# The first expert pair's up and down places, released and refilled in halves

## The chip, the cores and the metric

The kernel runs on one core of a Trainium2 chip. The metric is the device time of one launch in microseconds (us), as the median of several executions. Inputs are float32.

## What is computed

Two transformer blocks on one sequence of 256 tokens with a width of 1024. The change touches only the last part of the second block, its mixture of experts. Every token is sent to 2 of 32 experts, and each expert has three matrices of 2 MB (1024 x 512, 1024 x 512 and 512 x 1024), 201 MB in all:

```python
def _hierarchical_moe(h, w_group, w_expert, w_gate, w_up, w_down):
    ...
    def expert_block(args):
        xb, e = args
        return (jax.nn.silu(xb @ w_gate[e]) * (xb @ w_up[e])) @ w_down[e]

    y = lax.map(expert_block, (buf.reshape(n_blocks, MOE_BLOCK, d), block_expert)).reshape(cap, d)
    contrib = y[dest] * w_sorted[:, None].astype(y.dtype)
    return jnp.zeros((n, d), y.dtype).at[tok_sorted].add(contrib)
```

The result is scaled by a gate, added to the residual and normalised.

## The kernel before

The program is written out by hand for each engine, with semaphores between them. SP (SyncE) issues the loads of the weights in one fixed order, each behind a wait for the engine that frees its place; PE does the products; ACT and DVE evacuate, activate and scale; POOL does small work.

The 32 experts are taken as 16 pairs, since two experts with 64 token slots each share the 128 rows of TensorE. PE's part of pair p is `pair` in the tensor program. It does, in this order: the gate product (line 1389, 16 matmul calls, shown as 32 instructions), which ends in an increment of `s_eg`; the up product (line 1405), which ends in `s_eu`; the dispatch of the tokens of pair p + 1 (line 1333); transposes of the activated rows (line 1413); the combine of pair p - 1 (line 1350, from pair 1 on); transposes for the combine weights (line 1419); and the down product (line 1433), which ends in `s_edn`. ACT's `tokens` (line 1728) and DVE's (line 2313) copy the dispatched tokens, and ACT's line 1740 copies the transposed rows that the down product reads.

The weights lie in ten places of 16 KB per partition (`eslots`) and in one that is used a single time (`used_once`). `matrix(c, n)` is matrix c (0 gate, 1 up, 2 down) of expert n, so matrix (1,4) is the up matrix of expert 4, in pair 2. `matrix_number` counts them in the order of use, `slot_of` gives the place of each, and `requests_until` tells how many DMAs into that place must have landed before matrix m may be read (each DMA adds 16 to the place's `loaded` semaphore). `into` issues one whole load of 2 MB (line 666). Each load into a place waits until the matrix before it in the place is used up: for (1,7), for instance, until `s_edn` tells that pair 1's down product is done.

The first pair is special. Its gate product releases its two places in quarters: after every second of its eight k steps it adds one to `s_part`, SP waits for each count, and `quarter_into` (line 673) refills a quarter of each place, with matrices (2,3) and (0,4). [...] The up and down places of the first pair are refilled whole: (0,5) and (1,4) after `s_eu`, (1,5) and (2,4) after `s_edn`. The last pair's up and down matrices are loaded in halves (`halves_of_last`, line 692), and its down product adds a count to `s_part` when one of its two output halves is done, for which DVE waits.

The loads around the change, in SP's order, each behind the semaphore that it waits for: (2,3) and (0,4) `s_part` 1 to 4; (0,5), (1,4) `s_eu` 1; (1,5), (2,4) `s_edn` 1; (2,5), (0,6) `s_eg` 2; (0,7), (1,6) `s_eu` 2; (1,7) `s_edn` 2; (2,6), (2,7) `s_eg` 3; (0,8), (0,9) `s_eu` 3; (1,8), (1,9) `s_edn` 3; (2,8), (2,9) `s_eg` 4; and so on, six loads a pair.

Of the kernel before, what the change touches and what calls it, by code (L numbers as in the profile page):

```python
# [19 lines left out]
def two_block_kernel(nc, a, out):  # L20
# [22 lines left out]
    KE = FE // P  # L43
# [27 lines left out]
    ESLOT_N = 10  # L71
# [3 lines left out]
    QUARTERS = 4  # L75
# [16 lines left out]
    with ctx:  # L92
# [391 lines left out]
        def slot_of(m):  # L484

            if m == ESLOT_N:
                return ONCE
            return ESLOTS[m if m < ESLOT_N else (m - 1) % ESLOT_N]

        def requests_until(m):  # L490

            if m == ESLOT_N:
                return 2
            before_experts = N_MOE // LANES if slot_of(m) < LANES else 0
            in_quarters = QUARTERS - 1 if m > ESLOT_N and slot_of(m) in (slot_of(ESLOT_N + 1), slot_of(ESLOT_N + 2)) \
                else 0
            uses = 1 if m < ESLOT_N else (m - 1) // ESLOT_N + 1
            return before_experts + in_quarters + uses
# [5 lines left out]
        def expert_slot(u, c, e):  # L504

            return slot_of(matrix_number(u, c, e))
# [89 lines left out]
        def _(sp):  # L596
# [71 lines left out]
            def quarter_into(slot, src, quarter):  # L668

                rows = src.shape[1] // QUARTERS  # L670
                dst = expert_place(slot).rearrange("p (k n) -> p k n", k=src.shape[1])
                part = slice(quarter * rows, (quarter + 1) * rows)
                sp.dma_start(dst[:, part, :], src[:, part, :]).then_inc(loaded[slot], 16)
# [34 lines left out]
            for quarter in range(QUARTERS):  # L708
                sp.wait_ge(s_part, quarter + 1)
                quarter_into(expert_slot(1, 2, 1), matrix(2, 3), quarter)  # L710
                quarter_into(expert_slot(2, 0, 0), matrix(0, 4), quarter)
            into(expert_slot(2, 0, 1), matrix(0, 5), (s_eu, 1))
            into(expert_slot(2, 1, 0), matrix(1, 4), None)
            into(expert_slot(2, 1, 1), matrix(1, 5), (s_edn, 1))
            into(expert_slot(2, 2, 0), matrix(2, 4), None)
# [149 lines left out]
        def _(pe):  # L865
# [492 lines left out]
            def pair(p, u, r=None, last_one=False):  # L1358
# [48 lines left out]
                last.then_inc(s_eu, 1)  # L1407
# [21 lines left out]
                for f, c in order:  # L1429
# [6 lines left out]
                    if last_one and c == 0 and f == KE - 1:  # L1436
                        last.then_inc(s_part, 1)
                last.then_inc(s_edn, 1)
# [330 lines left out]
        def _(ve):  # L1769
# [546 lines left out]
            def pair(p, last_one=False):  # L2316
# [33 lines left out]
                if last_one:  # L2350
                    ve.wait_ge(s_part, QUARTERS + 1)
# [86 lines left out]
```

## Time and profile before

| | |
|---|---|
| Median of 3 runs | 1024.78 us |
| Lowest and highest | 1024.5 and 1026.88 us |
| The profiled execution's own time | 1026.15 us |
| Its span, first to last instruction | 1024.5 us |
| Mean granted TensorE clock over the span | 0.991 of full |
| Busy: PE, weight loads, DVE, ACT, POOL | 97%, 68%, 54%, 34%, 8% |
| Read from HBM | 310.47 MB |

The page cuts the span into 40 slices of 25.6 us; the expert stage fills those from the 23rd on. A timeline row has the start and the length of a group of instructions of one line, in us, and behind it in brackets the idle time of the engine before it and what ended that. Since matmuls overlap, the modelled end of a group can lie a little behind the start of the next. SP's rows are DMA issues: the time is that of the issue, not of the transfer. A DMA answer gives the time from the issue of a load to its landing, when all of it is in place.

### The profile page before, as it was taken

What the parts mean: (1) busy time and instruction counts of PE and PEld (TensorE: products, weight loads), DVE (VectorE), ACT (ScalarE), POOL (GpSimd) and SP (SyncE); (2) the same over time, 40 slices, a digit from 0 to 9 for tenths busy, and PEclk for the clock granted to TensorE, in tenths of its full rate; (3) what the DMA queues carried; (4) which work ended last, traced back from release to release, by engine and by line L of the source; (5) the groups of instructions that cost most, each with busy time, mean ns of one, the idle gap of its engine ahead of it and who ended that gap; (6) DMA issues with size and microseconds to landing.
All of it is one profiled execution on the core that took longest, in us unless ns stands there. A gap on an engine that the chain in (4) does not pass through costs nothing.

```text
span 1024.5 us, 15516 instructions
## 1 busy us (share of the span) xinstructions
PE 997.0 (97%) x6010; PEld 699.2 (68%) x6010; DVE 551.8 (54%) x1043; ACT 343.3 (34%) x572; POOL 79.6 (8%) x118
## 2 busy tenths in 40 slices
PE   8998999999999999999999999999999999999997
PEld 6897789989999998989965544444444444443442
DVE  8556689799899997748533622222222222222222
ACT  5555664464444554427250311111011111110112
POOL 7200110011011200300001000000000000000000
PEclk9999999999999999899999999999999999999999
DMA  8334176797879864245665899999999999999994
GB/s 299 123 124 164 46 257 237 264 345 276 307 300 320 301 219 164 83 166 208 265 265 176 317 361 429 423 429 428 427 427 427 427 427 429 429 427 428 429 424 190
DMA packets 60006, 312.15 MB, mean 305 GB/s; under 512 B 4117, under 2 KB 5498, under 8 KB 47418
## 3 DMA queue, kind: packets, MB, share of 16 engines
q1 hardware_dynamic: 52160, 284.83, 69.5%
q0 software_dynamic: 7392, 26.54, 7.2%
q8 instruction: 32, 0.52, 0.2%
q10 hardware_dynamic: 410, 0.16, 0.1%
q14 instruction: 12, 0.10, 0.0%
HBM read 310.47 MB, written 1.05 MB: 304 GB/s over the span
## 4 chain that ended last, share of the span: by engine, by line
PE 78%; DMA 8%; DVE 7%; issue 3%; ACT 2%; POOL 0%; DVEq 0%; SPq 0%
PE bank L1433 10%; PE bank L1405 10%; PE bank L1389 9%; PE bank L898 9%; PE bank L899 9%; PE bank L900 9%; PE bank L1333 6%; DMA eslots<-in_w_up 3%; DMA ring<-in_w_up 3%; PE bank L1045 3%; PE bank L1350 3%; DVE ring_r L1850 2%; DMA ring<-in_w_in 2%; PE bank L973 1%; PE bank L1011 1%
## 5 line engine op out<-in xcount | busy, mean ns | idle before, releaser
L898 PE MATMUL bank<-hT_r,ring_r 128*128 128x256 f32 x664 | 190.0, 286 | 2.7 <-DVE ring_r L1850 2.7
L900 PE MATMUL bank<-hT_r,ring_r 128*128 128x256 f32 x664 | 188.4, 284 | 0.0
L1850 DVE TENSOR_TENSOR ring_r<-ring,ring_r 128x2048 fp32r<-128x2048 f32 (+1 forms) x74 | 164.4, 2257 | 14.6 <-ACT ring_r L1511 14.2
L1511 ACT ACTIVATE ring_r<-ring 128x2048 fp32r<-128x2048 f32 (+1 forms) x74 | 136.5, 1888 | 37.4 <-DMA ring<-in_w_up 32.6
L899 PE MATMUL bank<-v_tok_r,ring_r 128*128 128x256 f32 x496 | 140.4, 283 | 0.0
L898 PEld LDWEIGHTS bank<-hT_r,ring_r 128*128 128x128 f32 x664 | 128.0, 193 | 4.0 <-issue 2.4
L900 PEld LDWEIGHTS bank<-hT_r,ring_r 128*128 128x128 f32 x664 | 127.9, 193 | 0.0
L1405 PE MATMUL bank<-eslots,scratch 128*64 128x512 f32 x512 | 114.5, 600 | 3.0 <-DMA eslots<-in_w_up 2.1
L1433 PE MATMUL bank<-eslots,scratch 128*64 128x512 f32 x496 | 113.5, 595 | 0.7 <-ACT scratch L1740 0.7
L1389 PE MATMUL bank<-eslots,scratch 128*64 128x512 f32 x512 | 112.7, 592 | 0.0
L899 PEld LDWEIGHTS bank<-v_tok_r,ring_r 128*128 128x128 f32 x496 | 95.2, 192 | 0.2
L2329 DVE TENSOR_TENSOR scratch<-scratch,bank 128x512 f32<-128x512 f32 x16 | 11.0, 688 | 156.5 <-PE bank L1405 156.5
L1405 PEld LDWEIGHTS bank<-eslots,scratch 128*64 128x64 f32 x512 | 38.6, 138 | 76.8 <-issue 73.9
L900 PE MATMUL bank<-ring_r,hn_r 128*128 128x512 f32 (+2 forms) x240 | 88.9, 370 | 0.0
L1389 PEld LDWEIGHTS bank<-eslots,scratch 128*64 128x64 f32 x512 | 37.1, 137 | 72.2 <-issue 72.1
L1433 PEld LDWEIGHTS bank<-eslots,scratch 128*64 128x64 f32 x496 | 35.6, 137 | 63.1 <-issue 61.3
L2341 DVE SCALAR_TENSOR_TENSOR scratch<-bank,scratch,post_ffn 128x512 f32<-128x512 f32 x32 | 22.6, 746 | 99.8 <-PE bank L1433 99.8
L1744 ACT ACTIVATE scratch_r<-scratch 128x512 fp32r<-128x512 f32 x32 | 20.2, 630 | 148.5 <-DVE scratch L2341 148.0
L1333 PEld LDWEIGHTS bank<-scratch,hn 128*128 128x128 f32 x512 | 58.4, 192 | 12.7 <-issue 12.2
L779 POOL TENSOR_TENSOR small<-small 128x1 f32<-128x1 f32 (+1 forms) x20 | 15.1, 758 | 638.2 <-DVE small L2402 453.0
L1728 ACT ACTIVATE scratch<-bank,small 128x128 f32<-128x128 f32 x64 | 18.2, 368 | 132.9 <-PE bank L1333 132.9
L1333 PE MATMUL bank<-scratch,hn 128*128 128x128 f32 x512 | 61.4, 278 | 0.0
(306 smaller groups left out, 1470.2 us busy)
## 6 DMA issues: line engine op xcount, KB each, us to landing
eslots<-in_w_gate SPq DMA_DIRECT2D x31, 2048.0 KB, 23.6
eslots<-in_w_up SPq DMA_DIRECT2D x30, 2048.0 KB, 18.8
eslots<-in_w_down SPq DMA_DIRECT2D x28, 2048.0 KB, 22.5
ring<-in_w_up SPq DMA_DIRECT2D x16, 2048.0 KB, 11.1
ring<-in_w_in SPq DMA_DIRECT2D x9, 2048.0 KB, 7.9
ring<-in_w_down SPq DMA_DIRECT2D x8, 2048.0 KB, 8.5
kT<-in_w_ada POOLq DMA_DIRECT2D x24, 512.0 KB, 7.2
ring<-in_w_out SPq DMA_DIRECT2D x4, 2048.0 KB, 8.2
```

The costliest lines, as they stand in the source:

```text
L898: pe.matmul(dst, lhs[0], rhs[0], start=start, stop=False, **flags)
L899: pe.matmul(dst, lhs[0], rhs[1], start=False, stop=False, **flags)
L900: return pe.matmul(dst, lhs[1], rhs[0], start=False, stop=stop, **flags)
L1045: last = pe.matmul(PS[PROJ_BANKS[1][t, c]][:, :], hT[:, k, t * P:(t + 1) * P], w[:, k % HALF_K, c * HALF:(c + 1) * HALF], start=(first and ...
L1333: last = pe.matmul(XB[k // 4][:, (k % 4) * P:(k % 4 + 1) * P], hn[:, t, k * P:(k + 1) * P], oneh[:, t, :], start=(t == 0), stop=(t == T - 1))
L1350: last = pe.matmul(ACC[2 * t + c][:, :], combT[:, t, :], ye[:, part, c * HALF:(c + 1) * HALF], start=False, stop=False, skip_group_check=True)
L1389: last = pe.matmul(GB[64 * e:64 * e + 64, :], xeT[:, k, 64 * e:64 * e + 64], weights(0, e, k), start=(k == 0), stop=(k == KD - 1))
L1405: last = pe.matmul(UB[64 * e:64 * e + 64, :], xeT[:, k, 64 * e:64 * e + 64], weights(1, e, k), start=(k == 0), stop=(k == KD - 1))
L1433: last = pe.matmul(XB[c][64 * e:64 * e + 64, :], eactT[:, f, 64 * e:64 * e + 64], weights(2, e, f)[:, c * HALF:(c + 1) * HALF], start=(f = ...
L1511: sc.activation(hi, raw, ACT.Copy).then_inc(s_whi, 1)
L1850: last = ve.tensor_tensor(lo, raw, hi, ALU.subtract)
L2341: ve.scalar_tensor_tensor(ye_sum[:, half], PS[4 + c][:, :], wslot, post_ffn[:, half], ALU.mult, ALU.mult).then_inc(s_yg, 1)
```

## The change

The first pair's up product raises `s_part` after k steps 3 and 7, its down product after f steps 1 and 3 (in each the second column half's matmul), so that `s_part` counts to eight in that pair. PE then waits for count six and raises `s_eu` with a nop, and for count eight and raises `s_edn` with a nop. SP waits for counts five and six and loads halves of (0,5) and (1,4), two DMAs of 1 MB behind each count; then for seven and eight, with halves of (1,5) and (2,4). `quarter_into` becomes `part_into` with the number of parts, `requests_until` counts one more DMA for the four places, and DVE's wait in the last pair goes from count five to nine.

```diff
-            in_quarters = QUARTERS - 1 if m > ESLOT_N and slot_of(m) in (slot_of(ESLOT_N + 1), slot_of(ESLOT_N + 2)) \
-                else 0
+            in_parts = 0
+            if m > ESLOT_N:
+                in_parts = {slot_of(ESLOT_N + 1): QUARTERS - 1, slot_of(ESLOT_N + 2): QUARTERS - 1,
+                            slot_of(ESLOT_N + 3): 1, slot_of(ESLOT_N + 4): 1,
+                            slot_of(ESLOT_N + 5): 1, slot_of(ESLOT_N + 6): 1}.get(slot_of(m), 0)
...
-            into(expert_slot(2, 0, 1), matrix(0, 5), (s_eu, 1))
-            into(expert_slot(2, 1, 0), matrix(1, 4), None)
-            into(expert_slot(2, 1, 1), matrix(1, 5), (s_edn, 1))
-            into(expert_slot(2, 2, 0), matrix(2, 4), None)
+            for half in range(2):
+                sp.wait_ge(s_part, QUARTERS + half + 1)
+                part_into(expert_slot(2, 0, 1), matrix(0, 5), half, parts=2)
+                part_into(expert_slot(2, 1, 0), matrix(1, 4), half, parts=2)
+            for half in range(2):
+                sp.wait_ge(s_part, QUARTERS + half + 3)
+                part_into(expert_slot(2, 1, 1), matrix(1, 5), half, parts=2)
+                part_into(expert_slot(2, 2, 0), matrix(2, 4), half, parts=2)
             into(expert_slot(2, 2, 1), matrix(2, 5), (s_eg, 2))
...
-                last.then_inc(s_eu, 1)
+                    if isinstance(p, int) and p == 0 and k % 4 == 3:
+                        last.then_inc(s_part, 1)
+                if isinstance(p, int) and p == 0:
+                    pe.wait_ge(s_part, QUARTERS + 2)
+                    pe.nop().then_inc(s_eu, 1)
+                else:
+                    last.then_inc(s_eu, 1)
...
-                    if last_one and c == 0 and f == KE - 1:
+                    first_pair_half = isinstance(p, int) and p == 0 and c == 1 and f % 2
+                    if (last_one and c == 0 and f == KE - 1) or first_pair_half:
                         last.then_inc(s_part, 1)
-                last.then_inc(s_edn, 1)
+                if isinstance(p, int) and p == 0:
+                    pe.wait_ge(s_part, QUARTERS + 4)
+                    pe.nop().then_inc(s_edn, 1)
+                else:
+                    last.then_inc(s_edn, 1)
...
-                    ve.wait_ge(s_part, QUARTERS + 1)
+                    ve.wait_ge(s_part, QUARTERS + 5)
```

SP's queue from the last quarter on, before the change (the name behind "waits" is the semaphore that the issue waits for):

```order
L673 DMA eslots<-in_w_gate 128x1024
L666 DMA eslots<-in_w_gate 128x4096 [waits s_eu]
L666 DMA eslots<-in_w_up 128x4096
L666 DMA eslots<-in_w_up 128x4096 [waits s_edn]
L666 DMA eslots<-in_w_down 128x4096
L666 DMA eslots<-in_w_down 128x4096 [waits s_eg]
```

And with the change (the lines are numbered three higher):

```order
L676 DMA eslots<-in_w_gate 128x1024
L676 DMA eslots<-in_w_gate 128x2048 [waits s_part]
L676 DMA eslots<-in_w_up 128x2048
L676 DMA eslots<-in_w_gate 128x2048 [waits s_part]
L676 DMA eslots<-in_w_up 128x2048
L676 DMA eslots<-in_w_up 128x2048 [waits s_part]
L676 DMA eslots<-in_w_down 128x2048
L676 DMA eslots<-in_w_up 128x2048 [waits s_part]
L676 DMA eslots<-in_w_down 128x2048
L669 DMA eslots<-in_w_down 128x4096 [waits s_eg]
```

Four whole loads have become eight of half the size, behind four waits instead of two; the load of (2,5) and all that follow it stand where they stood.

PE in the first pair, from the up product to the next pair's gate, before the change:

```order
L1405 MATMUL bank<-eslots,scratch 64x512 x15
L1333 MATMUL bank<-scratch,hn 128x128 [waits s_oneh,s_yV]
L1333 MATMUL bank<-scratch,hn 128x128 x15
L1413 MATMUL bank<-ident,scratch 128x128 [waits s_eact]
L1413 MATMUL bank<-ident,scratch 128x128 x3
L1419 MATMUL bank<-ident,scratch 128x128 [waits s_onehw]
L1419 MATMUL bank<-ident,scratch 128x128
L1433 MATMUL bank<-eslots,scratch 64x512 [waits loaded7,s_xeV,loaded1,s_xeA,s_eactT]
L1433 MATMUL bank<-eslots,scratch 64x512 x15
L1389 MATMUL bank<-eslots,scratch 64x512 [waits loaded6,loaded2,s_eactT,s_xeA]
```

And with it:

```order
L1412 MATMUL bank<-eslots,scratch 64x512 x15
L1340 MATMUL bank<-scratch,hn 128x128 [waits s_part,s_oneh,s_yV]
L1340 MATMUL bank<-scratch,hn 128x128 x15
L1426 MATMUL bank<-ident,scratch 128x128 [waits s_eact]
L1426 MATMUL bank<-ident,scratch 128x128 x3
L1432 MATMUL bank<-ident,scratch 128x128 [waits s_onehw]
L1432 MATMUL bank<-ident,scratch 128x128
L1446 MATMUL bank<-eslots,scratch 64x512 [waits loaded7,s_xeV,loaded1,s_xeA,s_eactT]
L1446 MATMUL bank<-eslots,scratch 64x512 x15
L1396 MATMUL bank<-eslots,scratch 64x512 [waits s_part,loaded6,loaded2,s_eactT,s_xeA]
```

No matmul moves. The dispatch and the next gate product each stand behind one more wait, the one for `s_part`.

## Rows read from the trace of the kernel before

**Rows 1.** The page: PE's busy time, and GB/s in the 40 slices

```profile
PE 997.0 (97%) x6010; PEld 699.2 (68%) x6010; DVE 551.8 (54%) x1043; ACT 343.3 (34%) x572; POOL 79.6 (8%) x118
...
GB/s 299 123 124 164 46 257 237 264 345 276 307 300 320 301 219 164 83 166 208 265 265 176 317 361 429 423 429 428 427 427 427 427 427 429 429 427 428 429 424 190
```

**Rows 2.** Timeline of PE, gate and up of pair 2

```profile
633.68 7.04 PE L1389 MATMUL bank<-eslots,scratch 128*64 128x512 f32 x32
640.54 7.04 PE L1405 MATMUL bank<-eslots,scratch 128*64 128x512 f32 x32
```

**Rows 3.** Timeline of PE, pair 0 and the gate of pair 1

```profile
580.09 7.09 PE L1389 MATMUL bank<-eslots,scratch 128*64 128x512 f32 x32
587.49 7.09 PE L1405 MATMUL bank<-eslots,scratch 128*64 128x512 f32 x32 [0.32 <-PE bank L1389]
594.51 3.84 PE L1333 MATMUL bank<-scratch,hn 128*128 128x128 f32 x32
...
599.73 7.09 PE L1433 MATMUL bank<-eslots,scratch 128*64 128x512 f32 x32 [0.72 <-ACT scratch L1740]
606.62 7.07 PE L1389 MATMUL bank<-eslots,scratch 128*64 128x512 f32 x32
```

**Rows 4.** DMA issued at 667.78, 949.57 and 976.42: size, us to landing

```profile
eslots<-in_w_down SPq DMA_DIRECT2D x1, 2048.0 KB, 11.6
...
eslots<-in_w_gate SPq DMA_DIRECT2D x1, 2048.0 KB, 39.7
...
eslots<-in_w_down SPq DMA_DIRECT2D x1, 1024.0 KB, 32.7
```

**Rows 5.** Timeline of PE, up of pairs 12 to 14, down of pair 15

```profile
911.04 7.09 PE L1405 MATMUL bank<-eslots,scratch 128*64 128x512 f32 x32
...
940.36 8.78 PE L1405 MATMUL bank<-eslots,scratch 128*64 128x512 f32 x32 [2.08 <-DMA eslots<-in_w_up]
...
969.77 7.09 PE L1405 MATMUL bank<-eslots,scratch 128*64 128x512 f32 x32 [0.48 <-issue]
...
1007.33 7.24 PE L1433 MATMUL bank<-eslots,scratch 128*64 128x512 f32 x32
```

**Rows 6.** Windows: busy us (x), granted clock, DMA share, GB/s

```profile
606.00:610.00 4.00, 4.00 (x20) 1.56 (x18) 3.04 (x7) 1.26 (x2) 0.00 (x0) 1.00 0.60 164
594.00:597.00 3.00, 3.00 (x26) 2.49 (x23) 0.69 (x1) 0.40 (x2) 0.00 (x0) 1.00 0.89 254
```

**Rows 7.** Timeline of SP: issues of (1,4), (1,5), (2,6) and (1,8)

```profile
594.98 0.43 SPq L666 DMA_DIRECT2D eslots<-in_w_up  x1
...
606.85 0.33 SPq L666 DMA_DIRECT2D eslots<-in_w_up  x1
...
640.75 1.06 SPq L666 DMA_DIRECT2D eslots<-in_w_down  x2
...
660.92 0.81 SPq L666 DMA_DIRECT2D eslots<-in_w_up  x2
```

**Rows 8.** DMA issued at 594.98, 606.85, 640.75, 660.92, then 529.24, 562.70

```profile
eslots<-in_w_up SPq DMA_DIRECT2D x1, 2048.0 KB, 12.8
...
eslots<-in_w_up SPq DMA_DIRECT2D x1, 2048.0 KB, 7.8
...
eslots<-in_w_down SPq DMA_DIRECT2D x1, 2048.0 KB, 9.0
...
eslots<-in_w_up SPq DMA_DIRECT2D x1, 2048.0 KB, 8.6
...
eslots<-in_w_down SPq DMA_DIRECT2D x1, 2048.0 KB, 7.5
...
eslots<-in_w_gate SPq DMA_DIRECT2D x1, 2048.0 KB, 7.8
```

**Rows 9.** Windows, as rows 6: after the idle time before 940.36

```profile
940.00:944.00 4.00, 3.64 (x10) 1.18 (x12) 0.00 (x0) 0.00 (x0) 0.00 (x0) 0.59 1.00 426
```

More of the change, by code:

```diff
@@ L494, in requests_until @@
             before_experts = N_MOE // LANES if slot_of(m) < LANES else 0
-            in_quarters = QUARTERS - 1 if m > ESLOT_N and slot_of(m) in (slot_of(ESLOT_N + 1), slot_of(ESLOT_N + 2)) \
-                else 0
+            in_parts = 0
[3 more added lines that the diff above has]
+                            slot_of(ESLOT_N + 5): 1, slot_of(ESLOT_N + 6): 1}.get(slot_of(m), 0)
             uses = 1 if m < ESLOT_N else (m - 1) // ESLOT_N + 1
-            return before_experts + in_quarters + uses
+            return before_experts + in_parts + uses
         def matrix_number(u, c, e):
@@ L666, in into, with part_into @@
                 sp.dma_start(dst, src).then_inc(loaded[slot], 16)
-            def quarter_into(slot, src, quarter):
-                rows = src.shape[1] // QUARTERS
+            def part_into(slot, src, n, parts=QUARTERS):
+                rows = src.shape[1] // parts
                 dst = expert_place(slot).rearrange("p (k n) -> p k n", k=src.shape[1])
-                part = slice(quarter * rows, (quarter + 1) * rows)
+                part = slice(n * rows, (n + 1) * rows)
                 sp.dma_start(dst[:, part, :], src[:, part, :]).then_inc(loaded[slot], 16)
@@ L709, in _ @@
                 sp.wait_ge(s_part, quarter + 1)
-                quarter_into(expert_slot(1, 2, 1), matrix(2, 3), quarter)
-                quarter_into(expert_slot(2, 0, 0), matrix(0, 4), quarter)
-            into(expert_slot(2, 0, 1), matrix(0, 5), (s_eu, 1))
-            into(expert_slot(2, 1, 0), matrix(1, 4), None)
-            into(expert_slot(2, 1, 1), matrix(1, 5), (s_edn, 1))
-            into(expert_slot(2, 2, 0), matrix(2, 4), None)
+                part_into(expert_slot(1, 2, 1), matrix(2, 3), quarter)
+                part_into(expert_slot(2, 0, 0), matrix(0, 4), quarter)
+            for half in range(2):
[6 more added lines that the diff above has]
+                part_into(expert_slot(2, 2, 0), matrix(2, 4), half, parts=2)
             into(expert_slot(2, 2, 1), matrix(2, 5), (s_eg, 2))
```

## The prediction

> **What bounds the kernel now.** I read the page first. PE is busy in 97% of the span, which by itself would say that only PE's work counts, but from the 25th slice to the 39th (from some 615 us) the DMA engines move 423 to 429 GB/s without a break [rows 1]. So the expert stage, which begins near 576 us, has two near-bounds. The timeline of PE gives the first: in a pair that waits for nothing the gate product starts 27.06 us after the one of the pair before (606.62, 633.68) [rows 2, 3]. The DMA answers give the second: the load issued at 667.78 landed after 11.6 us, at 679.4, and the one issued at 949.57 after 39.7, at 989.3 [rows 4]. Between them lie 63 loads of 2 MB (three of the same pair, then ten pairs of six), so one takes 309.9 / 63 = 4.92 us, and a pair's six 29.5 us. The DMA is 2.5 us a pair slower than PE, and PE lives on a head start that it uses up. The timeline near the end shows where that is gone [rows 5]: the up products at 940.36 and 969.77 start after 2.08 us (for DMA) and 0.48 us of idle time, and the last down product takes 7.24 us where 7.09 is usual, because its last half lands at 976.42 + 32.7 = 1009.1, just when it is wanted [rows 3 to 5]. **So the end of this kernel is set by when the stream of loads ends.** A us taken out of an early hole of the stream is a us at the end, if it stays out, up to a limit: PE by itself would start the product of 969.77 at 911.04 + 2 x 27.06 = 965.2, some 4.6 us earlier.
>
> **The holes.** The windows show two that the change aims at [rows 6]. From 606 to 610 us the DMA moved 164 GB/s where 428 is usual: 4 x (1 - 164/428) = 2.5 us missing. The queue had run dry, and the next load was issued only at 606.85, when the first pair's down product ended. From 594 to 597 it moved 254: 3 x (1 - 254/428) = 1.2 us. The busy share is 0.89 there, so part of it is the slow start of a new transfer.
>
> **Part 1: halves into the places of the first up.** Matrices (0,5) and (1,4) are issued when the up product ends, the second at 594.98 [rows 3, 7]. After the change their first halves go out when half of that product is done, 587.49 + 3.55 = 591.0, the second halves at 594.6. The quarters before them keep the engines busy until about 595, so the stream has no hole there: up to 1.2 us gained.
>
> **Part 2: halves into the places of the first down.** The first halves of (1,5) and (2,4) go out at 599.73 + 3.55 = 603.3 (plus the wait of part 4) instead of 606.85, while earlier loads still run. (1,4) landed at 594.98 + 12.8 = 607.8 and (1,5) at 606.85 + 7.8 = 614.7 [rows 7, 8]: 6.9 us between two landings where 4.9 is usual, so up to 2.0 us gained.
>
> **Part 3: smaller transfers.** Halves of 1 MB exist at the end of the kernel: the last eight take from 989.3 to 1009.1, 19.8 us for 8 MB, which four whole loads move in 19.7 [rows 4]. So eight more halves cost the stream 0.1 us, at most 0.3. SP issues eight DMAs in place of four, at 0.33 to 0.43 us each [rows 7]; that is hidden, as SP waits for PE between them.
>
> **Part 4: two new waits on PE.** After the first pair's up and its down product PE waits for its own last increment before a nop passes on `s_eu` and `s_edn`. The gate product has such a wait already: up starts 0.31 us after the gate's end (580.09 + 7.09), and 7.40 us after its start, against 6.86 in a later pair (633.68, 640.54) [rows 2, 3]. So it costs 0.54 there. Without a wait the dispatch starts 0.07 us before up's modelled end (594.51 against 594.58) and the next gate 0.20 us before down's (606.62 against 606.82). With 0.31 us behind the end they start 0.38 and 0.51 us later: **0.89 us in all**. The bounds are nothing, if a wait is over when PE reaches it, and 2 x 0.54 = 1.08. Behind these waits stand the dispatch, the transposes and the down product of PE, ACT's and DVE's tokens, which wait for the dispatch, and every later pair; PE has no idle time to absorb it until the stage's end. There it costs nothing by itself: PE waits 2.08 + 0.48 us for loads anyway.
>
> **Part 5: what becomes of the gain.** Loads (1,5) and (2,4) come up to 3.0 us earlier (1.2 + 2.0 - 0.2). But a later load is issued when PE frees its place, and PE is 0.89 us later, not earlier. So I follow each load as the later of two times: the landing before it + 4.9, and its own issue + what a load takes from a queue that has run dry. That second price is 7.5, 7.8 and 7.8 us in three rows [rows 8]; I take 7.8, that of 606.85, the nearest in time and an up matrix too. (2,4) lands at 616.6, 3.0 earlier. (2,6), issued at 640.75 + 0.89 = 641.6, can't land before 649.4; it was 640.75 + 9.0 = 649.8. So nearly all of the gain is lost again in a new hole: there was no free place to load into. (0,9), three loads on, lands at 664.1. (1,8), issued at 660.92 + 0.89 = 661.8, can't land before **669.6; it was 669.5** (8.6 after its issue, little more than from a dry queue) [rows 7, 8]. From there every load waits 5 us or more in the queue, PE's pace no longer matters to it, and the stream keeps what it has: 0.1 us later than before.
> The bounds: with 7.5 us (1,8) lands 0.2 earlier than it did; with waits that cost nothing it lands between 668.4 and 668.7, 0.8 to 1.1 earlier; with 1.08 us of waits 0.3 later.
> The Trainium skill (DMA: Bandwidth & Descriptors, Anatomy of one DMA) puts a transfer at about 2.0 us of fixed time plus its bytes at 436 GB/s, 6.8 us for 2 MB; the trace doesn't agree, with 7.5 to 7.8. By the page (1,8) would land at 668.6, and the sum would be 0.9 us faster instead of 0.1 slower.
>
> **Sum.** +0.1 us on the profiled execution's 1026.15 (1.65 of which lie around its span of 1024.5). That execution stands 1.4 us over the median of the runs shown; on the median of 1024.78 the forecast is **1024.9 us**. A measurement of this kernel can tell about 0.3% (3.1 us) from no change, and this is far inside.
>
> **The rivals.**
> A. *The holes stay closed.* If a load into a nearly dry queue landed 5 us after its issue, the 3.0 us would reach the end: 1021.8. For it: PE has the waits to give back. Against it: no row has less than 7.5, and PE frees the places no earlier. Chance 0.06, half of it beyond 0.3%.
> B. *The waits or the restart are cheaper.* With nothing for the waits 0.9 us is left at the end: 1023.9; with 0.89 of waits and the quickest landing 1024.6. For it: part of the gate's 0.54 may belong to its own place. Against it: up began 0.31 us behind the gate's end, idle. Chance 0.20; the 1023.9 that the page's fixed time gives falls under it.
> C. *Slower: a new wait drops TensorE's clock.* After the idle 2.08 us the granted clock was 0.59 of full on average from 940 to 944 us (the level of 1.2 GHz for most of it), and the product took 8.78 us, 1.74 more than 7.04 [rows 2, 5, 9]. If one of the new waits did that, (1,8) would be issued 1.74 us later still, and nothing makes it up: the end comes 1.8 us later than before, at 1026.6. For it: the idle time before dispatch is new. Against it: 0.32 and 0.72 us of idle time before 587.49 and 599.73 left products of 7.09 us, the full clock [rows 3]. It decides from a pause somewhere between 0.72 and 2.08 us on, and I expect 0.5. Chance 0.06; it passes 0.3% only if it comes twice.
> D. *The change doesn't do what it says:* the halves are issued early but the hole at 606 is there as before, and only the waits are left. The end is then set at (1,8) all the same, 1024.9. I put it with the forecast.
>
> **Chances and range.** Forecast (with D) 0.65, A 0.06, B 0.20, C 0.06, something else 0.03. All but half of A and most of the rest lie within 0.3%: faster 0.04, same 0.92, slower 0.04. The range takes in B, to 0.9 us faster, and C, to 1.8 slower, and as three runs of one kernel span 1024.5 to 1026.88 it goes from 1023.2 to 1026.9.
>
> **What would show it.** After the change: no hole from 606 to 610; the dispatch of pair 1 near 594.9 and the gate of pair 1 near 607.5; a new hole near 642; (2,6) landing near 649.4 and (1,8) near 669.6; the last half near 1009, and PE's wait before 940 shorter by the 0.89 us. If (1,8) lands before 668 and the last half before 1007.5, my step on the places is wrong.

## The result, and the profile after

The change makes the kernel slower by 0.2%: a median of 1027.65 us (1023.47 to 1030.24) against 1025.40 (1022.77 to 1028.59), 20 executions each, a ratio of 1.0020 with a 95% interval from 1.0010 to 1.0029. That is 2.0 us where 0.1 was forecast, and just outside the range of 1023.2 to 1026.9. A second and a third set of 12 executions gave 1.0015 (1.0000 to 1.0031) and 1.0007 (0.9993 to 1.0021). The profiled execution of the change took 1027.29 us, its span is 1025.9. One execution of the kernel before, 1121.4 us at a granted clock of 0.847, is left out everywhere.

The stage before the experts starts and ends by its own chance in each execution: the first gate product starts at 578.49 us here, at 580.09 in the profile before, and between 578.3 and 583.1 in the profiles of all runs. So in what follows I count from the start of the first gate product. By this clock the stage took 444.4 us before (to the end of the span) and takes 447.4 now.

The windows of the changed kernel: length, busy us (x) of PE, weight loads, DVE, ACT and POOL, granted clock, DMA share, GB/s.

```profile
592.00:595.00 3.00, 2.69 (x21) 1.84 (x18) 0.69 (x1) 0.00 (x0) 0.00 (x0) 1.00 1.04 433
606.00:610.00 4.00, 4.00 (x20) 1.69 (x22) 3.96 (x12) 1.26 (x2) 0.00 (x0) 1.00 1.01 418
640.00:642.00 2.00, 2.00 (x12) 0.61 (x10) 0.00 (x0) 0.60 (x1) 0.00 (x0) 1.00 0.67 164
660.00:664.00 4.00, 4.00 (x22) 1.38 (x20) 3.63 (x10) 1.26 (x2) 0.00 (x0) 1.00 0.88 332
```

Both holes of [rows 6] are closed, 433 and 418 GB/s in the place of 254 and 164. (In the place of the second a smaller one stands a little earlier: from 602 to 606 us 328 GB/s were moved, 0.9 us missing where it had been 2.5.) Two new ones have opened, at 640 and 660 us, as the forecast had it. They stand where (2,6) and (1,8) are issued. SP's timeline shows these issues, and the DMA answers for them how long each took to land:

```profile
640.11 0.80 SPq L669 DMA_DIRECT2D eslots<-in_w_down  x2
...
660.26 0.80 SPq L669 DMA_DIRECT2D eslots<-in_w_up  x2
```

```profile
eslots<-in_w_down SPq DMA_DIRECT2D x1, 2048.0 KB, 7.7
...
eslots<-in_w_up SPq DMA_DIRECT2D x1, 2048.0 KB, 9.0
```

(2,6) took 7.7 us from a dry queue, (1,8) 9.0. Counted from the first gate, (1,8) is issued at 81.8 us (80.8 before) and lands at 90.8 (89.4 before). The last half lands at 430.3 (429.1 before).

PE's timeline in the first pair, the answer to [rows 3]:

```profile
578.49 7.09 PE L1396 MATMUL bank<-eslots,scratch 128*64 128x512 f32 x32
585.89 7.09 PE L1412 MATMUL bank<-eslots,scratch 128*64 128x512 f32 x32 [0.31 <-PE bank L1396]
593.28 3.81 PE L1340 MATMUL bank<-scratch,hn 128*128 128x128 f32 x32 [0.30 <-PE bank L1412]
...
598.47 7.09 PE L1446 MATMUL bank<-eslots,scratch 128*64 128x512 f32 x32 [0.72 <-ACT scratch L1758]
605.97 7.09 PE L1396 MATMUL bank<-eslots,scratch 128*64 128x512 f32 x32 [0.41 <-PE bank L1446]
```

The dispatch starts 14.79 us after the gate (14.42 before), the next gate product at 27.48 (26.53 before): 0.37 and 0.58 us, 0.95 in all.

PE's timeline at the end, the answer to [rows 5], and the window behind the second wait, to [rows 9]:

```profile
910.73 7.09 PE L1412 MATMUL bank<-eslots,scratch 128*64 128x512 f32 x32 [0.44 <-issue]
...
940.05 7.09 PE L1412 MATMUL bank<-eslots,scratch 128*64 128x512 f32 x32 [2.09 <-DMA eslots<-in_w_up]
...
969.46 8.78 PE L1412 MATMUL bank<-eslots,scratch 128*64 128x512 f32 x32 [2.17 <-issue]
...
1008.70 7.09 PE L1446 MATMUL bank<-eslots,scratch 128*64 128x512 f32 x32
```

```profile
969.00:973.00 4.00, 3.54 (x10) 1.44 (x12) 0.00 (x0) 0.00 (x0) 0.00 (x0) 0.61 1.03 438
```

Here lies what I had not foreseen. Idle times of 2 us stand before both up products, and TensorE's clock can fall behind such a wait. Before, TensorE's clock fell to the 1.2 GHz level behind the wait for pair 13's up product (8.78 us). PE was 1.7 us later by that, but the next up product had to wait for its loads anyway, and its idle time shrank to 0.48 us: the drop cost nothing. Now the clock stays up at pair 13 and falls behind the wait for pair 14. Nothing after that waits for loads, so the 1.7 us go straight to the end: the last down product starts at 1008.70, its last half lands at 1008.8, before it is wanted, and it takes the plain 7.09 us. Of the 3.0 us that the stage is longer, 1.3 come from the later start of pair 14's up product and 1.7 from the slower clock behind it.

### The profile page after: what moved, and what is told of

Same layout as the page of the kernel before. It is cut to its first block, busy times and chain, and to the rows that moved or that the text cites. A ratio compares the mean times of both kernels' runs of the same rounds, so it can differ in the third digit from the quotient of the medians.

```text
span 1025.9 us, 15512 instructions
## 1 busy us (share of the span) xinstructions
PE 997.0 (97%) x6000; PEld 699.4 (68%) x6010; DVE 551.7 (54%) x1043; ACT 343.0 (33%) x572; POOL 78.9 (8%) x118
## 4 chain that ended last, share of the span: by engine, by line
PE 82%; DMA 7%; DVE 6%; issue 2%; ACT 2%; POOL 0%; SPq 0%; DVEq 0%
PE bank L905 11%; PE bank L907 10%; PE bank L906 10%; PE bank L1412 10%; PE bank L1446 10%; PE bank L1396 9%; PE bank L1340 6%; DMA eslots<-in_w_up 4%; PE bank L1052 3%; PE bank L1357 3%; DMA ring<-in_w_in 2%; PE bank L980 2%; DVE ring_r L1868 1%; DMA ring<-in_w_up 1%; PE bank L1018 1%
```

## The experiments

Theory **places**: the end follows the stream, and the stream is set when PE frees the place of (1,8). Theory **clock** or **cover**: in addition a drop of TensorE's clock now falls behind the last wait, which no later wait absorbs. Rivals: the smaller transfers make the stream slower; PE's time counts everywhere; the price sits in one half of the change. "Zeros" are four 512-column bf16 products of zeros, 1.04 us, into the bank that the up product overwrites, ahead of up products near the end.

The table has what the profiles show (one execution each, us from the start of the first gate product) and what the executions took. "Up 13" and "up 14" are the up products of pairs 13 and 14, with the idle time before them and their length. The end of the stage lies 54.6 to 55.1 us behind the start of pair 14's up product in all profiles without a drop behind it, and 56.2 to 56.4 in those with one.

| Kernel | (1,8) issued, landed | up 13: idle, length | up 14: start, idle, length | stage | ratio to before (95%) |
|---|---|---|---|---|---|
| before | 80.8, 89.4 | 2.08, 8.78 | 389.7, 0.48, 7.09 | 444.4 | |
| change, 1st set | 81.8, 90.8 | 2.09, 7.09 | 391.0, 2.17, 8.78 | 447.4 | 1.0020 (1.0010, 1.0029) |
| change, 2nd | 81.8, 90.2 | 2.02, 7.09 | 390.3, 2.19, 8.78 | 446.8 | 1.0015 (1.0000, 1.0031) |
| change, 3rd | 81.8, 90.0 | 1.88, 7.09 | 390.2, 2.17, 8.78 | 446.6 | 1.0007 (0.9993, 1.0021) |
| waits only, 1st | 81.8, 90.6 | 2.05, 7.09 | 390.3, 2.17, 7.09 | 445.0 | 1.0001 (0.9985, 1.0016) |
| waits only, 2nd | 81.8, 90.2 | 2.03, 7.09 | 390.3, 2.17, 8.78 | 446.6 | 1.0006 (0.9992, 1.0021) |
| up only | 81.2, 90.5 | 2.08, 8.78 | 390.3, 0.50, 7.09 | 445.0 | 0.9996 (0.9983, 1.0010) |
| down only | 81.5, 89.8 | 2.12, 7.09 | 390.2, 2.19, 7.09 | 444.8 | 0.9987 (0.9976, 0.9997) |
| halves, no waits | 80.8, 89.0 | 1.88, 7.09 | 389.2, 2.17, 7.09 | 444.0 | 0.9998 (0.9984, 1.0011) |
| halves and quarters, no waits | 80.3, 89.9 | 2.08, 8.78 | 390.0, 0.46, 7.09 | 444.9 | 0.9997 (0.9985, 1.0009) |
| waits in pair 4 | 80.8, 90.5 | 2.08, 8.78 | 390.6, 0.47, 7.09 | 445.3 | 1.0004 (0.9990, 1.0019) |
| before, 0.5 MB more | 80.8, 89.6 | 2.07, 7.09 | 391.1, 2.18, 8.78 | 447.3 | 1.0003 (0.9990, 1.0017) |
| before, zeros | 80.8, 90.2 | 0, 7.09 | 390.5, 1.22, 7.09 | 445.2 | 0.9997 (0.9985, 1.0008) |
| before, zeros at 8, 13 | 80.8, 90.0 | 0.15, 7.09 | 389.5, 2.17, 7.09 | 444.2 | 1.0003 (0.9987, 1.0018) |
| change, zeros | 81.8, 89.9 | 0, 7.09 | 390.2, 0, 7.09 | 445.0 | 0.9994 (0.9983, 1.0005) |
| change, zeros at 9, 14 | 81.8, 90.5 | 1.15, 7.09 | 390.5, 1.21, 7.09 | 445.4 | 1.0004 (0.9990, 1.0019) |
| waits only, zeros | 81.8, 89.8 | 0, 7.09 | 390.2, 0, 7.09 | 444.7 | 1.0014 (1.0003, 1.0025) |
| halves, no waits, zeros | 80.8, 90.0 | 0, 7.09 | 390.1, 0.89, 7.09 | 445.0 | 0.9991 (0.9977, 1.0005) |
| no waits at all, zeros | 80.3, 89.4 | 0, 7.09 | 389.6, 0.87, 7.09 | 444.7 | 0.9987 (0.9977, 0.9997) |
| 0.5 MB more, zeros | 80.8, 89.6 | 1.04, 7.09 | 391.6, 1.23, 7.09 | 446.3 | 1.0008 (0.9994, 1.0023) |

Single executions of one kernel differ by 4 to 7 us, so 12 of them give an interval of 1.0 to 1.6 us to either side; a single row of the last column tells little, and I pool kernels below. The ratios and the averages over all executions beside each other also differ by up to 1.1 us. "Down only" is 1.3 us faster than before by its ratio and 0.25 by the averages, "waits only, zeros" 1.4 us slower by its ratio and 0.4 by the averages. A difference of 1 us in one row is not shown by that row.

### 1. The waits without the halves

The PE side as in the change, `requests_until` and SP as before:

```diff
-            for half in range(2):
-                sp.wait_ge(s_part, QUARTERS + half + 1)
-                part_into(expert_slot(2, 0, 1), matrix(0, 5), half, parts=2)
...
+            into(expert_slot(2, 0, 1), matrix(0, 5), (s_eu, 1))
+            into(expert_slot(2, 1, 0), matrix(1, 4), None)
+            into(expert_slot(2, 1, 1), matrix(1, 5), (s_edn, 1))
+            into(expert_slot(2, 2, 0), matrix(2, 4), None)
```

> The kernel before with the change's two waits and nops on PE in the first pair, and all loads whole as before. Theory 'places' (the end is set by when the load of matrix (1,8) can be issued, which PE's third down product decides, so what delays PE in the first pair delays the end): the holes at 606 stay, (1,8) is issued 0.9 to 1.0 us later after the start of the first gate product than before (80.83 before, 81.8 here), the last half lands about 1 us later after that start, ratio 1.001 to 1.002, as with the whole change. Rival 'small transfers' (the eight halves make the stream slower and dry starts dearer, the waits are paid out of idle time at the end): ratio 1.000, last half within 0.3 us of before. Rival 'clock' (what is slow is a drop of TensorE's clock after the last wait for loads, in more executions than before): 1.000 to 1.002, with the stream's end as before and the product after the last wait taking 8.8 us.

> The waits without the halves once more, beside the change on the same chip: the one comparison that 12 executions each left open (1026.1 us on average for the waits alone, 1027.5 for the change). 'Places': the same time as the change in this batch within 0.7 us, both 1.0005 to 1.002. 'Both are needed' (the halves add their own price, by the two dry starts that they make at (2,6) and (1,8)): the waits alone within 0.5 us of the kernel before, 1 us or more below the change.

The issue of (1,8) is at 81.8 us in both profiles, and pair 14's up product starts at 390.3 us in both, as in the second and third profile of the change (390.3, 390.2): the closed holes leave no trace at the end. That is what "places" says. But the two profiles of this one kernel differ by 1.5 us in the length of the stage, and only by the clock. The first one's up product of pair 14:

```profile
969.21 7.09 PE L1407 MATMUL bank<-eslots,scratch 128*64 128x512 f32 x32 [2.17 <-issue]
```

The second one's:

```profile
969.37 8.78 PE L1407 MATMUL bank<-eslots,scratch 128*64 128x512 f32 x32 [2.17 <-issue]
```

The same idle time of 2.17 us, once without and once with a drop. By times the waits alone cost 0.1 and 0.6 us. The first, 1.0001, is a miss for "places", which wanted 1.001 to 1.002, and the number that "small transfers" wanted, though the stream ended 0.6 us later, which that theory doesn't have. The second is level with the change beside it (1.0006 and 1.0007), as "places" expected. The two together can't be told from either side.

### 2. The halves without the waits

The first half is released by a count of `s_part`, the second by `s_eu` or `s_edn` itself, which the last matmul raises as before:

```diff
+                sp.wait_ge(*((s_part, QUARTERS + 1), (s_eu, 1))[half])
...
+                sp.wait_ge(*((s_part, QUARTERS + 2), (s_edn, 1))[half])
...
+                    if isinstance(p, int) and p == 0 and k == 3:
+                        last.then_inc(s_part, 1)
+                last.then_inc(s_eu, 1)
```

> The change without its two waits: the first halves are released by a count of s_part, the second halves by s_eu and s_edn themselves, which the last matmul raises as before, so no nop and no wait on PE. Theory 'places': (1,8) is issued as before (80.8 us after the first gate's start) and lands 0 to 1 us earlier than before, new holes of the stream before (2,6) and (1,8) as in the change; ratio 0.999 to 1.000, faster than the change by 1 to 2 us. Rival 'small transfers': as the change, ratio 1.001 to 1.002, (1,8) and the last half later than before although issued at the same time.

In the other, the gate's last quarter is released by `s_eg` in the same way, and its nop goes too:

> As the halves without waits, and the first gate product loses its wait and nop too: its last quarter is released by s_eg itself. Theory 'places': PE is 0.5 us earlier from the first up product on, so (1,8) is issued 0.5 us earlier after the first gate's start than before (80.3) and the stream ends 0.5 to 1.3 us earlier; ratio 0.9985 to 0.9995. Rival 'small transfers': the release is earlier but the stream isn't, ratio 1.000 or more.

0.9998 and 0.9997: in the range of "places" and below the change in the first case, a little less than hoped in the second. Averages over 24 executions of the two are 1025.6 us with a standard error of 0.3, and 1027.3 with 0.3 over the 44 of the change. The kernel before, measured beside each, stands at 1025.5 to 1026.0 on average. So the halves as transfers aren't what costs; the 1.7 us between them come with the waits. The issue of (1,8) moved as expected (80.8, 80.3), but its landing took 8.2 us in one and 9.6 in the other.

### 3. The same waits where no place hangs on them

As 1, with `p == 4` in place of `p == 0`:

> As the kernel with the waits only, but the two waits stand in the fifth pair (pair 4), behind the release of (1,8), where the loads wait 5 us and more in the queue. Theory 'places': PE is 0.9 us later from there on, the loads come as before, PE's waits before the last up products shrink by 0.9 us, the end doesn't move: ratio 1.000. Rival 'PE's time counts everywhere': 0.9 us slower, ratio 1.001, the same as with the waits in the first pair. Rival 'clock': 1.000 or below, since a shorter wait at the end drops the clock less often.

1.0004, with an interval that holds 0 and 0.9 us. In the profile the up product of pair 13 waits 2.08 us and that of pair 14 0.47, as before [rows 5], and the last stretch is as before. But PE is 0.95 us later there and the loads happen to be 0.9 us later too, because (1,8) took 9.7 us from its issue to its landing, with the same loads and the same issue as before, where it took 8.6. That PE's 0.9 us would have gone into idle time had the loads come as before is likely, and not shown: the run doesn't decide between "places" and "PE's time counts everywhere" (by the averages it is 0.6 +- 0.5 us slower). It shows that a single profile's stream is uncertain by some 1 us.

### 4. Zeros ahead of the last up products

In pairs 8, 9, 13 and 14; the wait for `s_combT` is one that the up product has anyway:

```diff
+                if r is not None and u >= PERIOD + 3:
+                    pe.wait_ge(s_combT, p + 1)
+                    stay_awake(UB, 4)
                 if not last_one:
                     ready(1)
```

> The changed kernel once more, on the same chip and beside the same runs of the kernel before as the others of this batch. If the change's price is real: 1.001 to 1.003 again (1.5 to 2.5 us). If the waits' 0.9 us at the issue of (1,8) are all that is systematic: 1.0005 to 1.0015. In the profile the first gate's start to (1,8)'s issue is 81.8 us again; the time from its issue to its landing, 8.6 in the kernel before and 9.05 in the change, is expected anywhere from 8 to 10, since it was 9.7 in a kernel with the same loads as before and the same issue.

> The changed kernel with four 512-column bf16 products of zeros into the bank of the up product (which overwrites it), 1.03 us, ahead of the up products of pairs 8, 9, 13 and 14, where PE has time to give. Theory 'clock' (about 1.2 us of the change's price are drops of TensorE's clock after the last waits for loads, which no later wait covers): no idle time of 2 us before the up products of pairs 13 and 14, no half clock there, last half's landing to the end 15.3 us as in the kernel before and not 17.1, mean clock up by 0.001, and 1.0 to 1.7 us faster than the change. Rival 'stream only': the products of zeros hide in the wait and nothing changes, same time as the change; or they cost up to 1 us where PE arrives late.

> The kernel before with the same products of zeros and nothing else. Theory 'clock': the kernel before has drops too, in part of its executions uncovered, so 0.3 to 1.0 us faster, ratio 0.999 to 0.9997. Rival: 1.000 or up to 1 us slower.

The change with the zeros, at pair 14 (a window of 4 us, so the counts are those of the matmuls in it):

```profile
965.45 2.32 PE L1396 MATMUL bank<-eslots,scratch 128*64 128x512 f32 x10
967.69 1.04 PE L876 MATMUL bank<-zrow 128*128 128x512 bf16 x4
968.66 1.93 PE L1415 MATMUL bank<-eslots,scratch 128*64 128x512 f32 x7
```

No idle time, no drop. The change beside it ran at 1.0015, with the drop (8.78 us behind 2.19 of idle time), and the one with zeros at 0.9994, 2.1 us less, or 1.7 by the averages; the kernel before gained 0.3 us by its ratio and nothing by the averages. This is as "clock" expected: with the zeros the change and the kernel before are level (averages 1025.6 and 1025.7, 12 executions each), and without them they are 1.3 us apart (1027.3 over 44, 1025.9 over 182, standard errors 0.3 and 0.1; 1.6 if each set of the change is held against the kernel before beside it). The mean granted clock over all these executions is 0.9890 in the change, 0.9898 before, and 0.991 to 0.992 in both with zeros.

### 5. Which of the two waits

The zeros in one of the two pairs only, `u == PERIOD + 3` in the kernel before, `u == PERIOD + 4` in the change:

> The kernel before with the products of zeros ahead of the up products of pairs 8 and 13 only. Theory 'cover' (what the change lost is that TensorE's clock now drops at the wait before pair 14's up product, behind which no wait for loads can absorb the slower product, while in the kernel before it drops at pair 13's, where the next wait does): this kernel keeps the clock up at pair 13's and leaves a full wait of 2.1 us before pair 14's, so it should do to the kernel before what the change does, without touching the first pair: 0.7 to 1.7 us slower, ratio 1.0005 to 1.0017, a product of 8.8 us at pair 14 in the profile and 17.1 us from the last half's landing to the end. Rival 'first pair' (the price comes from the halves and waits of the first pair): ratio 1.000 or below, as with the products of zeros in both pairs (0.9997).

> The changed kernel with the products of zeros ahead of the up products of pairs 9 and 14 only. Theory 'cover': the uncovered drop goes, a drop at pair 13's is allowed and costs nothing, so as fast as with the products of zeros in both pairs: ratio 0.999 to 1.0002, 1.2 to 2 us faster than the change; 15.3 us from the last half's landing to the end. Rival 'first pair': as the change, 1.0015 to 1.002.

The first is a miss for "cover" by its expectation: 1.0003, where 1.0005 to 1.0017 was expected. A full wait of 2.17 us stood before pair 14's up product, as it was meant to, but the clock didn't fall:

```profile
938.44 7.09 PE L1408 MATMUL bank<-eslots,scratch 128*64 128x512 f32 x32 [0.15 <-DMA eslots<-in_w_up]
...
967.86 7.09 PE L1408 MATMUL bank<-eslots,scratch 128*64 128x512 f32 x32 [2.17 <-issue]
```

So a long last wait isn't enough. This one ended 389.5 us after the first gate, those with a drop behind them at 390.2 to 391.1; but 390.2 and 390.3 also occur without a drop (down only, waits only). The profiles show what else differs. In the stage before the experts TensorE runs at the 1.2 GHz level for a while, and the place where it returns to full isn't the same in all executions. In the change:

```profile
422.00:423.00 1.00, 1.00 (x7) 0.94 (x6) 0.00 (x0) 1.00 (x3) 1.00 (x1) 0.50 0.00 0
424.00:425.00 1.00, 1.00 (x10) 1.00 (x9) 1.00 (x4) 1.00 (x3) 1.00 (x1) 1.00 0.00 0
```

In the waits only, first set:

```profile
424.00:425.00 1.00, 1.00 (x7) 1.00 (x7) 1.00 (x4) 1.00 (x3) 0.04 (x1) 0.50 0.00 0
426.00:427.00 1.00, 1.00 (x11) 1.00 (x10) 1.00 (x3) 1.00 (x2) 0.00 (x0) 1.00 0.00 0
```

The return is at 423.75 us there and at 425.88 here, 154.7 and 153.0 us before the first gate. Counted from this return, the waits of about 2.17 us before pair 14's up product ended after 544.9 to 545.9 us in all five profiles in which the clock fell behind them, and after 543.2 to 544.3 in all four in which it stayed up. A pair earlier it is the same: the waits of 1.9 to 2.1 us before pair 13's ended after 514.2 to 515.4 us in the four profiles with a drop there, and earlier or later than that in the eight others, if only by 0.03 and 0.05 us in the two nearest. So by these twelve profiles a wait counts by where it lies against the clock's earlier changes, and not by its length alone. In the kernel before, pair 13's wait ended at 515.0, among those with a drop; in the three profiles of the change it is 0.4 to 1.3 us later, at 515.4 to 516.3, past them, so the clock stays up, the next wait has its full length, and that one ends at 544.9 to 545.7, among those with a drop. I read this from the profiles afterwards, and no run was made to test it.

The second is 1.0004, a little above the 0.999 to 1.0002 of "cover", and better than the change's average but not clearly. It doesn't separate the two waits either: the zeros at pair 9 make PE 1 us later from there on, so the wait before pair 13's up product was only 1.15 us.

### 6. A later stream without touching the first pair

In the kernel before, one more load into a place that is read no more, behind the loads of pair 4:

```diff
+            sp.dma_start(used_once[:, 0:D], w_edown[:, 0, 0, :]).then_inc(s_loaded_once, 16)
```

> The kernel before with one more load of 0.5 MB into a place that nobody reads any more, behind the loads of pair 4, so that all later loads land 1.2 us later and nothing else changes. Theory 'late stream' (the end follows the stream, whatever delays it, and a later stream moves the waits at the end to where a clock drop isn't covered): 1.2 us from the stream and 0.5 to 1.7 from the clock, ratio 1.0015 to 1.003, mean clock 0.001 lower than before. Rival 'stream only': 1.2 us, ratio 1.001 to 1.0015, clock as before. Rival 'first pair': PE has room, ratio 1.000.

> The same with the products of zeros ahead of the up products of pairs 8, 9, 13 and 14. Both theories of the stream: 1.2 us slower than the kernel before with the zeros (0.9997), so 1.0005 to 1.0013; 'late stream' expects the kernel without the zeros to be 0.5 to 1.7 us slower than this one, 'stream only' 0 to 0.4.

The profile does what "late stream" said, with nothing of the change in it: pair 14's up product starts at 391.1 us, and the clock falls behind its wait:

```profile
970.90 8.78 PE L1406 MATMUL bank<-eslots,scratch 128*64 128x512 f32 x32 [2.18 <-issue]
```

The stage took 447.3 us, as long as the change's. The times don't settle it: 1.0003 without and 1.0008 with the zeros, where 1.2 us of stream alone would be 1.0012, and their order is the reverse of the expected: for "late stream", which wanted 1.0015 to 1.003 without the zeros, the first is a miss. Both intervals hold 1.0012.

### 7. Up and down alone

`requests_until`, SP and PE of the change for one of the two products, the other as before:

> The change for the up places alone: halves of (0,5) and (1,4), one wait on PE. The issue of (1,8) comes 0.4 us later after the first gate's start (81.2), the hole at 606 stays. 'Places': ratio 1.0002 to 1.001, about 40 per cent of the change's price.

> The change for the down places alone: halves of (1,5) and (2,4), one wait on PE. The issue of (1,8) comes 0.5 to 0.6 us later (81.4), the hole at 606 is gone and new ones stand before (2,6) and (1,8). 'Places': ratio 1.0003 to 1.0012, about 60 per cent of the change's price; if the price were in the halves of the down matrices it would be all here, 1.0015 to 1.002.

(1,8) is issued at 81.2 and 81.5 us, as expected; the times are a miss, 0.9996 and 0.9987, the second faster than before by its ratio but hardly by the averages (0.25 +- 0.5 us). Neither profile has the uncovered drop. No price shows in either half by itself.

### 8. Without the waits, with the zeros

> The change without its two waits on PE, with the products of zeros in pairs 8, 9, 13 and 14, so that the stream alone sets the end. Theory 'places': (1,8) is issued 80.8 us after the first gate's start and lands 0.5 to 1 us earlier than in the change with the same products (89.86), ratio to before 0.9985 to 0.9995. Rival 'small transfers': no faster than the change with them (0.9994) or slower.

> The kernel with halves and quarters but no waits at all in the first pair, with the same products of zeros. Theory 'clock' with 'places': no drop at the end, stream at its earliest: 1.0 to 2.0 us faster than the kernel before, ratio 0.998 to 0.999. Rival 'stream only': as the same kernel without the products of zeros, 0.9995.

> The change's two waits without its halves, with the same products of zeros. Theory 'places': as the change with them, ratio 0.9992 to 1.0005, since the release of (1,8) is the same and what was gained by the halves is lost there. Rival 'the halves' gain survives in part': 0.5 to 1 us slower than the change with them. Rival 'waits are free': as the kernel before with them, 0.9997, which the first can't be told from by times of this spread; the issue of (1,8) at 81.8 and not 80.8 us decides it in the profile.

0.9991 and 0.9987 (0.9977 to 0.9997) for the halves without waits, 1.0014 for the waits without halves. The last is a miss for "places", which wanted at most 1.0005; its (1,8) is issued at 81.8 us, so the waits aren't free either. The averages are 1024.7 us over the 24 executions of the first two and 1026.1 over the 24 of the two kernels with waits and zeros (this one and the change), standard errors 0.3 each: the waits' 0.95 us of PE cost 1.4 +- 0.4 us even where no drop is left at these up products. (One of the first two also lacks the gate's wait, so the difference in PE's time is 1.2 us on average.) The kernel with no waits at all and the zeros beats both kernels: the one before by 1.3 us (0.3 to 2.4), the change by some 3 us. Only the down halves alone reached the same ratio, which their average doesn't bear out.

### 9. A third set of the change

> The change, beside it: 1.001 to 1.0025 if its price holds in a third set. In the profile a stream that ends 0.2 to 1.2 us later after the first gate's start than in the kernel before (429.07), and, if TensorE's clock drops at pair 14's up product again, 17.1 us from the last half's landing to the end, else 15.3 to 15.5.

1.0007, below the 1.001 that was expected, with an interval that holds it and 1.0, and with the drop at pair 14's up product in this profile too:

```profile
968.81 8.78 PE L1412 MATMUL bank<-eslots,scratch 128*64 128x512 f32 x32 [2.17 <-issue]
```

## Why the prediction was wrong

**Parts 1 and 2, right in the main.** Both holes closed, but (2,4) landed 2.1, 2.2 and 1.4 us earlier in the three profiles of the change, counted from the first gate, where 3.0 was forecast: a smaller hole at 602 to 606 us was left. It made no difference to the end.

**Part 3, right within its means.** The kernels with the halves and without the waits are no slower than before.

**Part 4, right in size, wrong in its cover.** 0.89 us forecast, 0.95 measured. I wrote that at the end it costs nothing by itself, and let it count only through the issue of (1,8), where I took a load from a dry queue (7.8 us in the place of 8.6) to make up for it. It doesn't: the 1.3 us that the change costs on average over 44 executions are all gone when the waits are gone. Nor did PE's wait before pair 13's up product shrink by the 0.89 us: it is 2.09 us, 2.08 before.

**Part 5, the step on the places, right in its mechanism and mis-sized.** The new holes stand where they were forecast. (2,6) was priced at 7.8 us from a dry queue and took 7.7. The 6.8 us that I estimated from the Trainium skill (DMA: Bandwidth & Descriptors, Anatomy of one DMA) aren't borne out by this either; the section gives its formula as a fit for loads that GpSimd issues, and these are issued by SP. (1,8) was priced at 7.8 too and took 9.0, 8.4 and 8.2 in the three profiles of the change. My rule of the later of two times gives 89.6 us after the first gate for the first of them (84.7 + 4.9 as well as 81.8 + 7.8), and it landed at 90.8. And the landing of before that I compared with was early for its kind: 8.6 us, against 8.8, 8.8, 9.2, 9.3 and 9.7 in five other profiles with the same loads before it and the same issue. With 0.9 to 1.0 us more at the issue, pair 14's up product starts on average at 390.4 us in the eight profiles with both waits, at 389.9 in the eight kernels without new waits in the first pair and without the extra load (the one before and seven more of the table). The last half lands 0.4 us later in the first eight than in the second (429.7 and 429.3). So the stream ends 0.4 to 0.5 us later, not 0.1. A price of one row stood where 8.0 to 9.7 us were measured.

**The sum, and what failed in it: "the end is set by when the stream of loads ends".** It is, but not by that alone: behind the last wait for loads comes 54.7 us of work that took 56.4 in all three profiles of the change and 54.7 in the one of before. The sum had no term for this; it stood at nothing, and it measured 1.7 us. Rival C had this mechanism and its price, 1.74 us, and put it in the wrong place: I looked for it behind the two new waits, where the idle time is 0.30 and 0.41 us and the clock stayed up, and not behind waits of 2 us that were there already. [rows 5] showed a drop behind a wait of 2.08 us and a wait of 0.48 us behind it; that the first explains the second, and that without it both waits are over 2 us, was there to be read. The 4.6 us by which I let PE be earlier there were read from the same rows and hold the drop's 1.7 us beside the idle time, which I didn't see.

What is shown: the drop behind the last wait, in all three profiles of the change, in one of two of the waits alone and in the kernel with more to load, and in none of the seven other profiles of kernels without zeros or with them at pair 13 alone; and that zeros in front of these waits take 1.7 to 2.1 us off the change and 0 to 0.3 off the kernel before. What is likely, and adds up, is 0.5 us of stream and the drop in more of the executions. Why the clock falls behind one wait of 2.17 us and not behind another is likely a matter of where the wait lies (section 5): a shift of 0.4 to 1.3 us moved the drop from a wait that another covers to one that nothing covers. That is luck of place, and another kernel may gain by such a shift as well as lose. What stays open is in how many executions it happens, and so why the waits alone (+0.4 +- 0.4 us on average over 24) and the stream made 1.2 us later (1.0003) cost less than this says. The spread of single executions is too wide for the runs made.

The forecast of 1024.9 missed by another 0.6 us because the median of the first three executions, 1024.78, lay under that of all twenty, 1025.40. Moved up by these 0.6 us the range would end at 1027.5, and 1027.65 would still lie outside. The executions of the kernel before span 5.8 us, of which three had shown 2.4.

## What to carry to other kernels

Filling an early hole of a stream of loads is worth nothing where the next loads can't be issued before the consumer frees their places; follow each load as the later of "the one before it" and "its own release", and expect that what delays the consumer there (here a nop behind a wait of PE for its own count) is paid at the end, in part or in full. A second half can be released by the semaphore that the last matmul raises anyway, without making PE wait. Where a kernel ends on waits for loads of about 2 us, look at the granted clock behind each, and at whether a later wait covers it; filling them with products of zeros cost nothing that could be measured here (1025.7 us on average with and without them in the kernel before).

## What the runs showed of the hardware that I had not expected

- The granted clock fell behind idle times of 2.08 to 2.19 us in nine of the twenty profiles, and stayed up behind idle times of 1.88 to 2.19 elsewhere; behind 1.53 us and less it never fell at these up products. When it fell, the product of 7.09 us took 8.78. Whether it fell went with where the wait lay, counted from the last return of the clock to full (section 5).
- The time from the issue of (1,8) to its landing, with 2.9 to 4.7 us of loads before it in the queue, ranged from 8.0 to 9.7 us for one and the same place in the program.
- A wait of PE for its own last increment cost 0.49 us between gate and up (7.40 us from start to start with it, 6.91 in the same pair without), 0.37 between up and dispatch and 0.58 between down and the next gate.
